# Halo sums by running the convolution past the block's end, three small works moved to GpSimd, silus and gate products in pairs

## The reference, cut to what matters

```python
D_MODEL, BATCH, SEQ = 1024, 8, 2048          # 2048 tokens per core
SSM_INNER, SSM_HEADS, SSM_GROUPS, SSM_STATE, SSM_CONV = 2048, 32, 8, 128, 4
FFN_DIM, FFN_CONV = 2816, 3

def causal_dwconv(x, w, bias):               # out[t] = sum_k w[k] * x[t - (W-1) + k]
    ...
def mamba2_mixer(h, ...):
    z, xBC, dt = split(h @ in_proj)
    xBC = silu(causal_dwconv(xBC, conv_w, conv_b))       # 32 chunks of 128 channels: x 16, B 8, C 8
    y = ssd_chunked(xs, dt, A, Bm, Cm) + xs * D          # state carried from chunk to chunk
    y = group_rms_norm(y * silu(z), gnorm, SSM_GROUPS)
    return y @ out_proj
def conv_ffn(x, ...):
    gate, val = split(rms_norm(x, norm_g) @ w_in)        # 22 chunks of 128 channels each
    return (silu(causal_dwconv(gate, conv_w, conv_b)) * val) @ w_down

x = x + mamba2_mixer(rms_norm(x), ...)
x = x + conv_ffn(x, ...)                                 # layer 0
k, v = shared keys and values of x;  x = x + sliding_window_sink_attention(q(x), k, v, sinks) @ w_o
x = x + conv_ffn(x, ...)                                 # layer 1
```

## Time and profile before

| | |
|---|---|
| median of three timed runs | 2178.62 us |
| the profiled execution, its own time | 2189.22 us |
| its span on the slowest core (core 2) | 2187.2 us |
| spans of the eight cores | 2154.8 to 2187.2 us |
| HBM read and written | 314.10 MB, 66.72 MB |
| DMA traffic of the core, mean | 149 GB/s |

### The profile page before, as it was taken

One profiled execution on the slowest core, in us unless ns is written; L12 is line 12 of the kernel. 1 busy time (PEld: TensorE's weight loads), 2 busy tenths in 40 slices (PEclk: granted clock), 3 DMA queues, 4 the chain that ended last, 5 costly groups with the idle time before them and its releaser, 6 DMA issues.

```text
span 2187.2 us, 34293 instructions; the slowest of 8 cores (2154.8 to 2187.2 us)
## 1 busy us (share of the span) xinstructions
PE 1918.7 (88%) x9710; PEld 859.6 (39%) x9896; DVE 1403.7 (64%) x2484; ACT 1258.9 (58%) x2124; POOL 169.1 (8%) x309
## 2 busy tenths in 40 slices
PE   4787799987798899998789999899789999987898
PEld 2333344433244344444334444444324444442344
DVE  2788478768677337667867725886867734655461
ACT  3489476558857335545895815566786733326431
POOL 0121110111011100000000100000000000000000
PEclk9899899999899997889999999999999999997899
DMA  9788689995299983444225444544224443431243
GB/s 212 166 189 180 156 194 237 222 226 136 59 201 251 204 240 112 136 131 126 78 69 155 163 138 161 161 143 134 90 58 136 145 133 128 158 122 53 68 154 135
DMA packets 107029, 325.89 MB, mean 149 GB/s; under 512 B 14304, under 2 KB 32224, under 8 KB 106848
## 3 DMA queue, kind: packets, MB, share of 16 engines
q1 hardware_dynamic: 91152, 266.55, 37.5%
q0 software_dynamic: 15696, 57.15, 16.7%
HBM read 314.10 MB, written 66.72 MB: 174 GB/s over the span
## 4 chain that ended last, share of the span: by engine, by line
PE 72%; ACT 10%; issue 7%; DVE 6%; DMA 5%; SPq 0%; ACTq 0%; DVEq 0%; POOL 0%; POOLq 0%
PE ps_ps L349 66%; PE ps_ps L362 4%; ACT sb_facc L381 3%; DMA sb_ring_fw<-w 2%; PE ps_ps L367 2%; ACT L381 2%; DVE sb_macc L397 2%; DMA sb_cm<-cm 1%; DMA w<-sb_ring_fw 1%; DMA sb_ring_mw<-w 1%; ACT sb_Eb L381 1%; ACT sb_macc L381 1%; ACT sb_mln L381 1%; ACT sb_msq L381 0%; ACT sb_fln L381 0%
## 5 line engine op out<-in xcount | busy, mean ns | idle before, releaser
L349 PE MATMUL ps_ps<-sb_hF,sb_ring_fw 128*128 128x512 bf16 x2750 | 655.7, 388 | 21.3 <-DVE sb_facc L397 7.4
L349 PE MATMUL ps_ps<-sb_uF,sb_ring_fw 128*128 128x512 bf16 x1941 | 467.7, 384 | 17.5 <-ACT sb_facc L381 7.3
L349 PE MATMUL ps_ps<-sb_hM,sb_ring_mw 128*128 128x512 bf16 (+1 forms) x1522 | 410.7, 404 | 58.6 <-DVE sb_macc L397 19.1
L349 PEld LDWEIGHTS ps_ps<-sb_hF,sb_ring_fw 128*128 128x128 bf16 x2816 | 276.6, 100 | 353.9 <-issue 82.7
L397 DVE SCALAR_TENSOR_TENSOR sb_macc<-ps_ps,sb_cst,sb_macc 128x511 f32<-128x511 f32 (+2 forms) x384 | 284.5, 744 | 16.3 <-PE ps_ps L349 1.9
L349 PEld LDWEIGHTS ps_ps<-sb_uF,sb_ring_fw 128*128 128x128 bf16 x1984 | 192.0, 99 | 245.0 <-issue 41.4
L397 DVE SCALAR_TENSOR_TENSOR sb_facc<-ps_ps,sb_cst,sb_facc 128x511 f32<-128x511 f32 x352 | 260.0, 745 | 17.6 <-PE ps_ps L349 5.7
L381 ACT ACTIVATE sb_facc<-ps_ps,sb_cst 128x512 f32<-128x512 f32 x204 | 154.2, 764 | 192.2 <-PE ps_ps L349 178.9
L381 ACT ACT_TABLE_LOAD x176 | 225.8, 1283 | 59.7 <-PE ps_ps L349 36.3
L349 PEld LDWEIGHTS ps_ps<-sb_hM,sb_ring_mw 128*128 128x128 bf16 (+1 forms) x1568 | 152.2, 103 | 248.5 <-issue 126.3
L386 DVE TENSOR_TENSOR sb_xT<-sb_xT,ps_ps 128x512 f32<-128x512 f32 x96 | 65.6, 687 | 234.1 <-PE ps_ps L349 222.3
(11 more groups left out here) (148 smaller groups left out, 2137.7 us busy)
## 6 DMA issues: line engine op xcount, KB each, us to landing
sb_ring_fw<-w SPq DMA_DIRECT2D x228, 512.0 KB, 3.5
sb_ring_mw<-w SPq DMA_DIRECT2D x99, 512.0 KB, 4.4
sb_ring_fw<-w POOLq DMA_DIRECT2D x76, 512.0 KB, 10.1
w<-sb_ring_fw SPq DMA_DIRECT2D x76, 512.0 KB, 9.4
sb_ring_mw<-w POOLq DMA_DIRECT2D x33, 512.0 KB, 8.4
w<-sb_ring_mw SPq DMA_DIRECT2D x33, 512.0 KB, 6.0
sb_Er<-er_scr SPq DMA_DIRECT2D x32, 512.0 KB, 6.4
out<-sb_uF SPq DMA_DIRECT2D x16, 512.0 KB, 3.5
```

Of the source, the lines that this page charges most:

```text
L349: return self.add("pe", lambda e: e.matmul(out, lhsT, rhs, start=start, stop=stop), [lhsT, rhs] + ([] if start else [out]), [out], cost=ma ...
```

## The change

The convolution now writes its taps over all 512 input columns and so runs n columns past the block's end: `acc` gets 4 more columns, GpSimd clears n of them first, and what stands there afterwards is the sum that the next block needs. GpSimd then adds the fix columns at the block's start (after the taps now, and not before them) and copies the n columns into `fix`. The halo copies on ScalarE and both `hfix` computations go. `xE` and `prevB` are computed by GpSimd. The silus of x0 and x1, of B and C, of z0 and z1 (where the banks are neighbours), and of gates 2k and 2k + 1 are one instruction of 1024 elements each, and so are the products of value chunks 2k and 2k + 1. For that, gates rotate over the first half of `ids` and values over the second half, and an even value chunk first asks for the record of the pair product before it. The scheduler's modelled costs of GpSimd copies and of memsets change.

```diff
     def copy(self, out, in_, eng="dve"):
-        return self.add(eng, lambda e: e.tensor_copy(out, in_), [in_], [out], cost=150.0 + 0.55 * _n(out))
+        return self.add(eng, lambda e: e.tensor_copy(out, in_), [in_], [out], cost=150.0 + (0.55 if eng == "dve" else 1.0) * _n(out))
     def memset(self, ap, val, eng="dve"):
-        return self.add(eng, lambda e: e.memset(ap, val), [], [ap])
+        return self.add(eng, lambda e: e.memset(ap, val), [], [ap], cost=100.0 + 0.5 * _n(ap))
...
-    macc = K.sb("macc", [128, 4, TB], F32)
+    macc = K.sb("macc", [128, 4, TB + 4], F32)
-    facc = K.sb("facc", [128, 4, TB], F32)
+    facc_t = K.sb("facc", [128, 4, TB + 4], F32)
...
-    def conv(acc, pb, taps, bias, fix, halo):
+    def conv(acc, pb, taps, bias, fix):
         n = len(taps) - 1
-        K.act(acc, pb, AF.Identity, bias=bias, scale=taps[n])
-        K.act(halo, pb[:, TB - n:TB], AF.Copy)
-        K.tt(acc[:, 0:n], acc[:, 0:n], fix, OP.add)
+        K.memset(acc[:, TB:TB + n], 0.0, eng="pool")
+        K.act(acc[:, 0:TB], pb, AF.Identity, bias=bias, scale=taps[n])
         for k in range(n - 1, -1, -1):
             s = n - k
-            K.stt(acc[:, s:TB], pb[:, 0:TB - s], taps[k], acc[:, s:TB], OP.mult, OP.add)
+            K.stt(acc[:, s:TB + s], pb, taps[k], acc[:, s:TB + s], OP.mult, OP.add)
+        K.tt(acc[:, 0:n], acc[:, 0:n], fix, OP.add, eng="pool")
+        K.copy(fix, acc[:, TB:TB + n], eng="pool")
...
                     if i >= 4:
-                        silu_q.append(lambda: K.act(ybuf[:, 2 * g + i - 4, :], ps[:, bk, :], AF.Silu))
+                        hs["z", i] = bk
                         if i == 5:
+                            b4 = hs["z", 4]
+                            if bk == b4 + 1:
+                                silu_q.append(lambda: K.act(ybuf[:, 2 * g:2 * g + 2, :], ps[:, b4:b4 + 2, :], AF.Silu))
...
-                        dst = xcb[:, g % 2, i, :] if i < 2 else BCb[:, g % 2, i - 2, :]
-                        silu_q.append(lambda: K.act(dst, acc, AF.Silu))
+                        if i % 2:
+                            dst = xcb[:, g % 2] if i == 1 else BCb[:, g % 2]
+                            silu_q.append(lambda: K.act(dst, macc[:, i - 1:i + 1, 0:TB], AF.Silu))
...
                     K.tt(xE[:].rearrange("p a (h d) -> p a h d", d=64), xtok[:].rearrange("p a (h d) -> p a h d", d=64),
-                         tokS[:, :, 4 * g:4 * g + 4].unsqueeze(3).to_broadcast([128, 4, 4, 64]), OP.mult)
+                         tokS[:, :, 4 * g:4 * g + 4].unsqueeze(3).to_broadcast([128, 4, 4, 64]), OP.mult, eng="pool")
...
                     K.tt(prevF[:, gs], stmp[:], ps[:, bk, 0:256], OP.add)
-                    K.act(prevB[:, gs], prevF[:, gs], AF.Copy)
+                    K.copy(prevB[:, gs], prevF[:, gs], eng="pool")
...
-            bk_ = Banks(ids)
+            bg_, bv_ = Banks(ids[:len(ids) // 2]), Banks(ids[len(ids) // 2:])
...
                     def post():
-                        conv(acc, ps[:, bk, :], ...)
-                        silu_q.append(lambda: K.act(uF[:, j, :], acc, AF.Silu))
+                        conv(facc_t[:, j % 4, :], ps[:, bk, :], ...)
+                        if j % 2:
+                            k = j % 4 - 1
+                            silu_q.append(lambda: K.act(uF[:, j - 1:j + 1, :], facc_t[:, k:k + 2, 0:TB], AF.Silu))
...
             def val(j):
                 def f():
+                    if j % 2 == 0 and j > 0:
+                        FL.ensure(hv["u"])
...
+                    if j % 2 == 0:
+                        hv["vb"] = bk
+                        return
+                    b0 = hv["vb"]
                     def post():
...
-                        K.tt(uF[:, j, :], uF[:, j, :], ps[:, bk, :], OP.mult)
+                        K.tt(uF[:, j - 1:j + 1, :], uF[:, j - 1:j + 1, :], ps[:, b0:b0 + 2, :], OP.mult)
                     hv["u"] = later(2, post)
```

More of the change, by code:

```diff
@@ L747, in build @@
     ps = K.psum("ps", [128, 8, 512], F32)
+    facc = facc_t[:].rearrange("p a n -> p (a n)")[:, 0:4 * TB].rearrange("p (a n) -> p a n", a=4)
     hkvT = uF
@@ L793, in build @@
     K.dma("sp", SR[:].rearrange("p a b n -> p (a b n)"), src_d, "c4")
-    for z in (halo_f, fix_f, fix_m, prevF, prevB):
+    for z in (fix_f, fix_m, prevF, prevB):
         K.memset(z[:], 0.0)
@@ L986, in f @@
                     j = 2 * g + i if i < 2 else (16 + g if i == 2 else 24 + g)
-                    acc = macc[:, i, :]
                     def post():
-                        conv(acc, ps[:, bk, :], [C(f"cw{k}", j) for k in range(4)], C("cb", j), fix_m[:, j, :], halo_m[:, j, :])
-                        dst = xcb[:, g % 2, i, :] if i < 2 else BCb[:, g % 2, i - 2, :]
-                        silu_q.append(lambda: K.act(dst, acc, AF.Silu))
+                        conv(macc[:, i, :], ps[:, bk, :], [C(f"cw{k}", j) for k in range(4)], C("cb", j), fix_m[:, j, :])
+                        if i % 2:
+                            dst = xcb[:, g % 2] if i == 1 else BCb[:, g % 2]
+                            silu_q.append(lambda: K.act(dst, macc[:, i - 1:i + 1, 0:TB], AF.Silu))
                     later(1, post)
@@ L1135, in hfix @@
         def hfix():
-            hl = halo_m
-            def m(o, k, hi):
-                K.tt(o, C(f"cw{k}"), hl[:, :, hi], OP.mult, eng="pool")
-            for o, terms in ((0, ((0, 0), (1, 1), (2, 2))), (1, ((0, 1), (1, 2))), (2, ((0, 2),))):
-                for n, (k, hi) in enumerate(terms):
-                    if n == 0:
-                        m(fix_m[:, :, o], k, hi)
-                    else:
-                        m(fixt[:], k, hi)
-                        K.tt(fix_m[:, :, o], fix_m[:, :, o], fixt[:], OP.add, eng="pool")
             if b + 1 < NBLK:
@@ L1213, in f @@
                     w = t16(fring.get(key))
-                    bk = bk_()
+                    bk = bg_()
                     for kc in range(8):
@@ L1218, in f @@
                         fring.free(key)
-                    acc = facc[:, j % 4, :]
                     def post():
-                        conv(acc, ps[:, bk, :], [C(f"fcw{l}_{k}", j) for k in range(3)], C(f"fcb{l}", j),
-                             fix_f[:, l, j, :], halo_f[:, l, j, :])
-                        silu_q.append(lambda: K.act(uF[:, j, :], acc, AF.Silu))
+                        conv(facc_t[:, j % 4, :], ps[:, bk, :], [C(f"fcw{l}_{k}", j) for k in range(3)], C(f"fcb{l}", j), fix_f[:, l, j, :])
+                        if j % 2:
+                            k = j % 4 - 1
+                            silu_q.append(lambda: K.act(uF[:, j - 1:j + 1, :], facc_t[:, k:k + 2, 0:TB], AF.Silu))
                         if j % 4 == 3 or j == NFC - 1:
@@ L1234, in f @@
                     w = t16(fring.get(key))
-                    bk = bk_()
+                    bk = bv_()
                     for kc in range(8):
@@ L1257, in hfix @@
                 FL.ensure(hv["u"])
-                hl, fx = halo_f[:, l], fix_f[:, l]
-                t = fixt[:, 0:NFC]
-                K.tt(fx[:, :, 0], C(f"fcw{l}_0"), hl[:, :, 0], OP.mult, eng="pool")
-                K.tt(t, C(f"fcw{l}_1"), hl[:, :, 1], OP.mult, eng="pool")
-                K.tt(fx[:, :, 0], fx[:, :, 0], t, OP.add, eng="pool")
-                K.tt(fx[:, :, 1], C(f"fcw{l}_0"), hl[:, :, 1], OP.mult, eng="pool")
                 if l == 0:
```

9 lines of the change are left out of this document (5 added, 4 removed).

## The result

The change made the kernel slower: 2227.65 us (median of 4 runs) against 2179.43 us beside it (4 runs of the kernel before), ratio 1.0224 with a 95% interval of 1.0176 to 1.0271, some 49 us. The prediction, 2158 us and a range to 2194, was wrong in sign. The profiled execution took 2229.16 us, its span 2227.8 us on core 6. Ratios leave out runs in which one half of the chip ran at a lower clock; the medians in microseconds may hold such runs. A difference between two ratios is as uncertain as both intervals together.

The account below looks back on a forecast made before the run. PE, busy 88%, stands still 242 us waiting for whichever of VectorE or ScalarE is late. Gains of 35 us, less 10 + 2 + 3 for pairs and the hop, leave 20: 2178.6 to 2158 us, range 2122 to 2194.

Parts of the forecast that it names:

- The state's path: prevB on GpSimd before the next stmp: a step 1.9 us against 1.4, at most 58 us, taken as zero.
- The sum's rule, r/(1 - r): PE's standstill follows the load r of the more loaded engine as r/(1 - r); gains over the stages together 35 us.
- The convolution: Halo copies and fix additions leave ScalarE and VectorE: per mixer block 5.3 and 5.2 us, per block's FFNs 7.3 and 7.2.
- Value pairs: In the weaves' FFNs, the pair product frees an even value's bank later: 66 times 0.15 us, 10 us lost.
- strong rival 1: VectorE does both gate taps before the pair product, even values wait 1.16 us, 66 times: 2226 us; chance 0.09.
- The lock: xE on GpSimd holds VectorE operations with two SBUF inputs: 16 us, plus 4 for small ones; bounds 0 and 67.
- ScalarE's load: Over four blocks ScalarE loses 143 us of 1259, from halo copies, prevB and paired silus; to 1115 us.
- rival 2: xE holds VectorE, additions after the taps hold silus behind DMAs; the 35 falls to 15, less 15: 2178 us; chance 0.12.
- rival 4: The planner's new order works against the change: ten more table loads a weave, 38 us on ScalarE; about 2180; chance 0.07.
- The DMA queue of the first weave: In block 0, casting DMAs waiting in GpSimd's queue hold up its small operations: a few us; first weave's gain halved to 6.

Follow-up runs that it names:

- b_dummy: Kernel before, with GpSimd also copying prevF into a tile nobody reads, ahead of the next stmp; prevB stays on ScalarE: ratio 1.0102.
- b_prevB: Kernel before with prevB on GpSimd, plus the change's modelled planner costs: ratio 1.0140.
- c_dve: Changed kernel with the convolution's memset, fix addition and copy into fix on VectorE instead of GpSimd: ratio 1.0211.
- conv_mid: Kernel before with silu pairs, xE on GpSimd and the running-on convolution, its fix addition on VectorE ahead of the taps: ratio 1.0112.
- b_val: Kernel before with the value pairs and both bank rotations, plus the change's modelled planner costs and wider acc tiles: ratio 1.0066.
- u_val: Changed kernel with single value products again and gates and values in one rotation over all banks: ratio 1.0141.
- u_prevB: Changed kernel with prevB alone back on ScalarE: ratio 1.0080.
- u_xE: Changed kernel with xE alone back on VectorE: ratio 1.0223.
- b_prevB_dve: Kernel before with prevB made by VectorE right behind prevF, nothing else changed: ratio 1.0251.
- b_silu_xE: Kernel before with silu pairs and xE on GpSimd, plus the change's modelled planner costs and wider acc tiles: ratio 0.9930, 2168.66 us.

## Why the prediction was wrong

- **The step that failed first: "The state's path ... I take zero."** The working was right up to there, the step longer by 0.4 to 0.5 us and its bound 58 us. It measured 1.4%, 31 us. I chose zero because an average of 7 us between steps (mixer 0; 16 in the weaves) covers 1.9. The average hid the bursts: within a group the median step is 2.65 us and a quarter take less than 1.9, as long as the path itself. A copy ahead of stmp alone cost 22 us (b_dummy, the planner's new order included); 9 us of the 31 lie beyond it. What PE waited for moved with it: in b_prevB its waits for prevF and prevB on the slowest core were 34 us in the rows shown, against 12 before. The bound I allowed on the other side, a gain of 0.41 a step without ScalarE's queue, did not show: prevB started sooner (0.26 against 0.54 us after prevF) and the kernel lost.
- **The sum's rule, r/(1 - r), failed too.** Both loads fell in each weave, and PE's stops rose: by 7 us in the second weave (10 by weight loads) where 8 less were forecast, and the clock took 9 more. b_prevB takes prevB's 53 us off ScalarE and loses 1.4%; c_dve puts the 912 small operations on VectorE (83 us more busy) at no cost that can be seen. The runs fit a standstill that follows which queue holds the next operation of a serial path, not the load of the queues. Without this rule no gain of 35 us was left in the sum. The sum also had no term for the clock.
- **The convolution, forecast as a gain (its operations were 50 of the 102 us and 50 of the 143), cost 0.9 to 1.1%, 19 to 25 us.** Neither the engine of its small operations (c_dve) nor the place of the fix addition (conv_mid) explains it. Whether it is the memset or addition as links in the chain of one chunk, or the order that the planner makes from them, stays open. It was not tried with halo copies kept and only the memset added.
- **Value pairs: sign and place right, size too small, mechanism not seen.** 10 us forecast in the weaves and none in the last rest; 14 to 18 measured by b_val and u_val, 8 in u_prevB. PE's wait for the product, from which the term was worked out, stayed at some 3 to 4 us in before, b_val and after, so what the pairs cost by stays open. The strong rival 1 (77 us) did not happen. The Trainium skill ("Perfetto Trace Analysis", "Optimizing Scalar/DVE Operations") has that breaking instructions up may let work end sooner where neither engine is saturated; these pairs agree in sign (+0.4 to +0.8%), silu pairs on top of xE do not (-0.5%).
- **The lock: mechanism right, its price not to be seen.** VectorE's Cs, tile views as the earlier trace rows, went to 2.297 us, as forecast ("up to 2 or 3 us"), its median unchanged:

```profile
L386 DVE TENSOR_TENSOR sb_Cs<-sb_Er,sb_BCb x64: 671/682/2297, 87.1 to 1783.3; 128x1024 bf16<-128x1024 bf16 x64
L397 DVE SCALAR_TENSOR_TENSOR sb_macc<-ps_ps,sb_cst,sb_macc x384: 719/744/755, 48.2 to 1764.9; 128x512 f32<-128x512 f32 x192
```

  The taps, with one input in PSUM, still never exceed 0.76. VectorE's load fell 45 us less than forecast, part of it the longer two-input products; and u_xE says that none of it costs time.
- **ScalarE's load.** Its rows fell by some 160 us when summed (table loads 20 of them), near the 143 forecast, but the union by 99: in the timeline before, a halo copy starts 0.11 us before the end of the activation ahead of it (1103.09 against 1103.20), so the union counts only the rest of its 0.17. I had added durations where the page counts a union.
- **GpSimd "gives the gain back" (rival 2) and the order (rival 4).** Table loads went down, from 176 to 160, not up by ten a weave, so rival 4's stated price is wrong for after; in b_prevB (190) and b_prevB_dve (200) they rose. Its other half, that a new order alone costs time, was not tested. The DMA queue of the first weave, which I had feared, was no place of the loss: that weave grew by 2.8 us, the second by 17.5.

What remains unsettled: the cause in the convolution and in the value pairs, why prevB is dear on VectorE too, why the silu pairs change sign, and what share of each price is the planner's new order.

## What to carry to other kernels

Before moving an operation to an idle engine, ask what serial path passes through that engine's queue, and at which spacing its steps come in a burst, not on average. A dummy operation in that place prices it in one run, with whatever the planner changes in answer. Lower busy shares were no gain here, where PE stopped for latencies. Take a bundle of edits apart both ways, from before and from after: here two of its parts together make the kernel 0.7% faster (b_silu_xE), and the whole makes it 2.2% slower.

## What the runs showed of the hardware

The lock goes both ways, and can starve GpSimd. Timeline of after, GpSimd and VectorE (a line's number at its end counts instructions joined in it):

```profile
1041.12 4.05 DVE L397 SCALAR_TENSOR_TENSOR sb_uF<-sb_xT,sb_cst,sb_fln 128x512 bf16<-128x512 f32 x6
1041.39 5.15 POOL L401 COPY sb_fix_m<-sb_macc 128x3 f32<-128x3 f32 x1 [0.80 <-DVE sb_macc L397]
1045.09 1.40 DVE L397 SCALAR_TENSOR_TENSOR sb_ybuf<-sb_ybuf,sb_cst,sb_mln 128x512 bf16<-128x512 bf16 x2
```

Its tile view beside that of prevB, as the earlier trace rows:

```profile
L401 POOL COPY sb_fix_m<-sb_macc x128: 179/188/5149, 52.2 to 1765.8; 128x3 f32<-128x3 f32 x128
...
L401 POOL CAST sb_prevB<-sb_prevF x128: 386/396/1267, 108.1 to 1805.8; 128x256 bf16<-128x256 f32 x128
```

A copy of three columns, 0.188 us at the median, took 5.15 us: it ended (1041.39 + 5.15 = 1046.54) when eight VectorE operations with two SBUF inputs had ended (1045.09 + 1.40 = 1046.49), which followed each other without a gap. Such waits lift the mean of its group to 470 ns.

The Trainium skill ("SBUF — State Buffer", "Who interferes with whom") says that whichever of the two comes second blocks; the trace agrees, and shows that it may stay blocked over a row of VectorE instructions.

Smaller prices: GpSimd casts 256 columns of float32 in 0.396 us (median; VectorE 0.316, ScalarE's mean 0.413), clears 2 or 3 columns in 0.101, and multiplies 1024 bf16 columns in 1.90 (median), where VectorE takes 1.22. An activation of 1024 elements from float32 in SBUF takes 1.054 us, from PSUM 1.016.
